# A hybrid streaming encoder step: gates a unit later, norm sums behind the mLSTM gates, rows turned among v's units

## What is computed

```python
def _trunk(x, p, cache, w):                      # cut
    for li in range(2):
        hn = _rmsnorm(h, norm_mix_g[li])
        # layer 0: RG-LRU and windowed attention behind one input projection
        # layer 1: mLSTM (matrix memory, chunks of 64)
        h = h + mixer(hn)
        h = h + _swiglu(_rmsnorm(h, norm_ffn_g[li]), ffn_w_in[li], ffn_w_out[li])
        h = h + jax.nn.sigmoid(h @ ple_w_gate[li]) * (p[li] @ ple_w_proj[li])
    return _rmsnorm(h, final_g), states

def _rglru(u, h0, w_r, b_r, w_i, b_i, lam):      # layer 0, u is behind a causal convolution
    r = jax.nn.sigmoid(_block_diag(u, w_r) + b_r)
    i = jax.nn.sigmoid(_block_diag(u, w_i) + b_i)
    log_a = -8.0 * r * jax.nn.softplus(-lam)
    a = jnp.exp(log_a)
    bx = jnp.sqrt(-jnp.expm1(2.0 * log_a)) * (i * u)
    # h[t] = a[t] * h[t-1] + bx[t]

proj = _rmsnorm(x, norm_mix_g[1]) @ w_in         # layer 1
u, v, o, gates = jnp.split(proj, [1024, 2048, 3072], axis=-1)
ig, lf = gates[..., :4] + b, jax.nn.log_sigmoid(gates[..., 4:] + b)
```

## Time and profile before

| | us |
|---|---|
| median of 3 runs | 2843.92 (2843.08 to 2844.82) |
| the profiled execution | 2844.14 |
| its span, first to last instruction | 2842.4 |
| PE busy | 2729.6 (96%) |
| DVE busy | 1476.1 (52%) |
| POOL busy | 949.9 (33%) |
| ACT busy | 600.7 (21%) |
| mean granted TensorE clock | 0.982 |

### The profile page before, as it was taken

One profiled execution on the slowest core, in us unless ns is written; L12 is line 12 of the kernel. 1 busy time (PEld: TensorE's weight loads), 2 busy tenths in 40 slices (PEclk: granted clock), 3 DMA queues, 4 the chain that ended last, 5 costly groups with the idle time before them and its releaser, 6 DMA issues.

```text
span 2842.4 us, 40945 instructions
## 1 busy us (share of the span) xinstructions
PE 2729.6 (96%) x17240; PEld 2672.7 (94%) x17240; DVE 1476.1 (52%) x2332; ACT 600.7 (21%) x1266; POOL 949.9 (33%) x439
## 2 busy tenths in 40 slices
PE   7999999999999999998999988799999999999996
PEld 7798899999999999998999977699999999999996
DVE  7956474444444444658663056546444444444565
ACT  3434331000000000223122145312000000000042
POOL 5222044433333333333433310024433333333430
PEclk9999999999999999999999999899999999999998
DMA  4101011111111111113122221301111111111111
GB/s 145 33 23 61 32 60 51 47 46 52 46 45 45 45 45 45 45 45 122 45 75 85 91 78 45 151 30 51 54 45 45 45 45 45 45 45 45 53 38 61
DMA packets 57830, 160.09 MB, mean 56 GB/s; under 512 B 7340, under 2 KB 28332, under 8 KB 56368
## 3 DMA queue, kind: packets, MB, share of 16 engines
q1 hardware_dynamic: 31056, 109.79, 12.3%
q10 hardware_dynamic: 26592, 47.70, 4.6%
HBM read 137.07 MB, written 20.40 MB: 55 GB/s over the span
## 4 chain that ended last, share of the span: by engine, by line
PE 90%; DVE 6%; ACT 3%; issue 1%; DMA 0%; ACTq 0%; DVEq 0%
PE ps L413 28%; PE ps L415 28%; PE ps L414 28%; PE ps L819 1%; PE ps L619 1%; PE ps L589 1%; PE ps L856 1%; DVE xl L907 1%; DVE uc L1178 1%; DVE hb L1489 1%; PE ps L601 0%; DVE cs L1463 0%; PE ps L858 0%; ACT kw L1926 0%; DVE rstd L900 0%
## 5 line engine op out<-in xcount | busy, mean ns | idle before, releaser
L413 PE MATMUL ps<-xh,wh 128*128 128x352 f32 x3432 | 1122.3, 327 | 21.3 <-DVE xl L907 14.3
L414 PE MATMUL ps<-xl,wh 128*128 128x352 f32 x3432 | 1114.4, 325 | 0.0
L415 PE MATMUL ps<-xh,wl 128*128 128x352 f32 x3432 | 1114.0, 325 | 0.0
L464 POOL TENSOR_TENSOR wh<-raw,seeds 128x1024 fp32r<-128x1024 f32 x208 | 422.3, 2030 | 1807.6 <-PE ps L415 1779.9
L413 PEld LDWEIGHTS ps<-xh,wh 128*128 128x128 f32 x3432 | 651.8, 190 | 26.2 <-issue 13.9
L414 PEld LDWEIGHTS ps<-xl,wh 128*128 128x128 f32 x3432 | 651.9, 190 | 2.1 <-issue 0.3
L415 PEld LDWEIGHTS ps<-xh,wl 128*128 128x128 f32 x3432 | 651.7, 190 | 0.0
L466 POOL TENSOR_TENSOR wl<-raw,wh 128x1024 fp32r<-128x1024 f32 x208 | 529.5, 2546 | 16.3
L1023 DVE TENSOR_TENSOR tmpa<-ps,rstd 128x352 f32<-128x352 f32 x132 | 69.1, 524 | 719.0 <-PE ps L415 710.8
L413 PE MATMUL ps<-hh,wh 128*128 128x352 f32 x1056 | 340.4, 322 | 0.0
L415 PE MATMUL ps<-hh,wl 128*128 128x352 f32 x1056 | 340.0, 322 | 0.0
(11 more groups left out here) (263 smaller groups left out, 2497.6 us busy)
## 6 DMA issues: line engine op xcount, KB each, us to landing
raw<-wstream SPq DMA_DIRECT2D x208, 512.0 KB, 3.6
vod<-stage ACTq DMA_DIRECT2D x72, 128.0 KB, 1.9
vb<-vod ACTq DMA_DIRECT2D x9, 512.0 KB, 4.0
ob<-vod ACTq DMA_DIRECT2D x9, 512.0 KB, 3.7
x<-xT ACTq DMA_DIRECT2D x3, 1408.0 KB, 11.7
x<-xT ACTq DMA_DIRECT2D x2, 2112.0 KB, 8.2
xsave<-x ACTq DMA_DIRECT2D x1, 4224.0 KB, 11.4
x<-xsave ACTq DMA_DIRECT2D x1, 4224.0 KB, 14.4
```

The source lines that it names most:

```text
L413: pe.matmul(out, whi, mhi, start=first, stop=False)
L414: pe.matmul(out, whi, mlo, start=False, stop=False)
L415: return pe.matmul(out, wlo, mhi, start=False, stop=last)
L464: pool.tensor_tensor(hi, raw[:, r, :], zero, ALU.add).then_inc(hi_made, 1)
```

## The change

Five edits:

1. Layer 0: `lru_gates(0)` stands after unit 12 instead of 11, and POOL splits block 6 only once conv(0) is done (`uc_ready`).
2. ScalarE's `gates(t)` begins with a one-column sigmoid that waits for nothing, ahead of the waits.
3. The transposes of v alternate between banks 6 and 7, so that only the ninth waits for a copy.
4. Norm ni = 2: all three sums stand behind the three units of the mLSTM gates' block; roots and reciprocals move behind the last highs and lows. POOL splits B1_GATE + 1 once the lows of two tiles are done, B1_GATE + 2 once all are.
5. `rows_to_columns` stands inside the first pair of v's blocks, ahead of its fourth token tile, instead of ahead of the pair.

```diff
-            later = {B0_FFN + 2: "ffn0", B1_FFN + 2: "ffn1"}
+            later = {B0_FFN + 2: XLN["ffn0"] + KT * NT, B1_FFN + 2: XLN["ffn1"] + KT * NT,
+                     B1_GATE + 1: XLN["mix1"] + KT * 2, B1_GATE + 2: XLN["mix1"] + KT * NT}
                 if b in later:
-                    pool.wait_ge(xl_ready, 1 + XLN[later[b]] + KT * NT)
+                    pool.wait_ge(xl_ready, 1 + later[b])
+                if b == 6:
+                    pool.wait_ge(uc_ready, 1)
@@ tail_phase (PE)
-                    if u == first or u == first + 4:
+                    if ni != 2 and u in (first, first + 4):
                         norm_sum(ni, (u - first) // 4)
@@ dense (PE)
-                    if tt == 1 and sums is not None:
-                        norm_sum(sums, NT - 1)
@@ transpose_v (PE)
-                    if j == 4:
+                    if j == 8:
                         pe.wait_ge(v_ready, 1)
-                    if j == 8:
-                        pe.wait_ge(v_ready, 2)
-                    mm = pe.transpose(ps[0:n, 7, (j % 4) * P:(j % 4 + 1) * P], vt[:, j * P:j * P + n], ident[:, :])
+                    mm = pe.transpose(ps[0:n, 6 + j // 4 % 2, (j % 4) * P:(j % 4 + 1) * P], vt[:, j * P:j * P + n], ident[:, :])
@@ IN0 loop (PE)
-                if u == 11:
+                if u == 12:
                     pe.wait_ge(m0_in, 16 * 5)
-                if u in (11, 14, 17):
-                    lru_gates((11, 14, 17).index(u))
+                if u in (12, 14, 17):
+                    lru_gates((12, 14, 17).index(u))
@@ layer 1 (PE)
-            dense(B1_GATE % NW, B1_GATE, FREE0["g1"] - 6, OFF["g1"], XLN["mix1"], 2)
+            dense(B1_GATE % NW, B1_GATE, FREE0["g1"] - 6, OFF["g1"], XLN["mix1"])
+            for tt in range(NT):
+                norm_sum(2, tt)
             dense_loop("u1", B1_U, KT)
-            (the rows' 53 matmuls and their two waits)
+            def rows_to_columns():
+                (the same)
                         for j in range(CH):
+                            if pair == 0 and j == 3:
+                                rows_to_columns()
@@ tail_phase (DVE)
-                        if u == 20:
+                        if u == 20 and ni != 2:
                             rstd_of(ni, 0)
-                    rstd_of(ni, 1)
-                    rstd_of(ni, 2)
+                    for tt in range(0 if ni == 2 else 1, NT):
+                        rstd_of(ni, tt)
@@ tail_norm (ACT)
-                    if u == 19 or u == 23:
+                    if ni != 2 and u in (19, 23):
                         root(ni, (u - 19) // 4)
-                        root(ni, 2)
+                        for tt in range(0 if ni == 2 else 2, NT):
+                            root(ni, tt)
@@ gates (ACT)
             def gates(t):
+                act.activation(seeds[:, 7:8], seeds[:, 0:1], ACT.Sigmoid)
                 if t >= 2:
                     act.wait_ge(h_ready, t - 1)
@@ values (ACT)
-                    (copies of v from bank 7)
+                    (copies of v from bank 6 + j, the ninth from bank 6)
```

More of the change, by code:

```diff
@@ L506, in tail_phase, with dense @@
                     first = 18 if ni < 4 else 17
-                    if u == first or u == first + 4:
+                    if ni != 2 and u in (first, first + 4):
                         norm_sum(ni, (u - first) // 4)
-            def dense(slot, b, free, bank0, xl_at=None, sums=None):
+            def dense(slot, b, free, bank0, xl_at=None):
                 pe.wait_ge(raw_free, split_count(b))
                 for tt in range(NT):
-                    if tt == 1 and sums is not None:
-                        norm_sum(sums, NT - 1)
                     pe.wait_ge(acc_free, free + tt + 1)
@@ L770, in _ @@
             ple(0, B0_PLE)
-            dense(B1_GATE % NW, B1_GATE, FREE0["g1"] - 6, OFF["g1"], XLN["mix1"], 2)
+            dense(B1_GATE % NW, B1_GATE, FREE0["g1"] - 6, OFF["g1"], XLN["mix1"])
+            for tt in range(NT):
+                norm_sum(2, tt)
             dense_loop("u1", B1_U, KT)
[L775 to L788, removed]
+            def rows_to_columns():
+                pe.wait_ge(rows_ready, 1)
+                pe.wait_ge(c_in, 16 * 4)
+                for cc in range(CH):
+                    for q in range(4):
+                        r = (0, 5, 4, 1)[q]
+                        pe.transpose(ps[:, 6, (cc * 4 + q) * 4:(cc * 4 + q + 1) * 4],
+                                     rows[:, r, cc * P:(cc + 1) * P], ident[0:4, 0:4])
+                for h in range(H):
+                    mm = pe.matmul(ps[:, 6, 256 + CH * h:256 + CH * (h + 1)], sel[:, h, :], rsmall[:, 32:32 + CH],
+                                   start=True, stop=True)
+                for cc in range(CH):
+                    n = P if cc < CH - 1 else TS
+                    mm = pe.transpose(ps[0:n, 6, 320 + 4 * cc:324 + 4 * cc], rstd[0:4, cc * P:cc * P + n], ident[0:4, 0:4])
+                mm.then_inc(cols_done, 1)
             for half in range(2):
@@ L1727, in values @@
                 if j < 2:
-                    act.activation(vtok[:, 4 * j + 1:4 * j + 5, :].rearrange("p a d -> p (a d)"), ps[:, 7, :],
+                    act.activation(vtok[:, 4 * j + 1:4 * j + 5, :].rearrange("p a d -> p (a d)"), ps[:, 6 + j, :],
                                    ACT.Copy).then_inc(v_ready, 1)
                 else:
-                    act.activation(vtok[0:TS, 10, :], ps[0:TS, 7, 0:P], ACT.Copy).then_inc(v_ready, 1)
+                    act.activation(vtok[0:TS, 10, :], ps[0:TS, 6, 0:P], ACT.Copy).then_inc(v_ready, 1)
             gates(0)
```

## The result

The changed kernel takes 2823.26 us (median of 4 runs, 2817.26 to 2824.80), the kernel before 2843.62 (4 runs, 2843.08 to 2844.82). The ratio is 0.992, with a 95% interval of 0.991 to 0.993: faster by 20 us. The prediction said 2820.7, between 2813.5 and 2829.5. The profiled execution took 2824.18 us, with a span of 2822.4, so it is 19.96 us shorter than the one of before (2844.14).

The account below looks back on a forecast made before the run. PE was busy 2729.6 of 2842.4 us, so only its waits and low-clock time could be won. Gains of 9.6 + 10.7 + 3.0 = 23.3 us gave 2820.7 us, range 2813.5 to 2829.5.

Parts of the forecast that it names:

- Part C: mLSTM rows to columns behind three of v's units: wait covered, small matmuls and next unit at full clock, 9.6 us gained.
- the small matmuls at 2.4 GHz: Among v's units: the 53 small matmuls would take 3.6 us at full clock instead of 6.5.
- rival 4: Four new pauses or thin stretches each bring a low-clock period costing about 6.8 us; slower, 2848 us; chance 0.02.
- lower bound, 6.7: Rows to columns: gain of 6.7 us if the small matmuls keep 6.5 us because their pace is not the array's.
- Part B: Layer 1's norm sums behind the mLSTM gates, splits held: 12.8 us lost time removed, less new waits; 10.7 us gained.
- The 0.3 us for the third norm sum: Layer 1's norm: the third sum needs the first root, so PE would wait 0.3 us.
- Part A: Layer 0's gates: moved splits only move their cost; gains from table loads and v's transposes, 3.0 us in all.
- Rival 1: Layer 0's gates pay in full, log1p and conv(1) not held by the moved splits: 2816.1 us; chance 0.13.
- rival 3: Layer 0's first gates stay bound by something other than conv(0), gaining nothing: 2823.7 us; chance included in the forecast's 0.70.
- conv(1): Layer 0: block 8's split delays this convolution's end to 88.8 from 85.2; PE waits 7.5 us before gates 1.
- the row: Table loads: the trace shows 1.28 us each without the drain; the forecast used this, not the skill's extra 1.38.
- Rival 2: New waits replace those removed in layer 1's norm and the rows to columns: 2828.2 us; chance 0.13.

Follow-up runs that it names:

- e1_rows: Kernel before with only the rows' small matmuls moved inside v's first pair of blocks, behind three units: 2838.11 us, ratio 0.9975.
- e4_norm_nohold: Kernel before with only the layer 1 norm sums moved behind the mLSTM gates, without the two waits that hold GpSimd's splits: 2844.86 us, ratio 0.9997.
- e9_24: Changed kernel with the split of block B1_GATE + 1 held until all 24 lows are done instead of 16: 2818.21 us, ratio 0.9907.
- e5_nohold6: Changed kernel without GpSimd's wait for conv(0) ahead of splitting block 6: 2821.06 us, ratio 0.9916.
- e2_norm: Kernel before with only the layer 1 norm sums moved behind the mLSTM gates and the two splits held: 2836.55 us, ratio 0.9967.
- e3_gates: Kernel before with only the layer 0 changes (gates 0 later, block 6 held, sigmoid table ahead, two banks for v's transposes): 2840.46 us, ratio 0.9986.
- r14_after: The changed kernel measured again, unaltered, on the chip of three later kernels: 2822.12 us, ratio 0.9919 against the kernel before.
- e13_later_only: Changed kernel with layer 0's gates 0, 1, 2 after units 12, 15, 18 and v's transposes after 22, log1p left in place: 2819.73 us, ratio 0.9912.
- e12_best: Changed kernel with early log1p, later gates and transposes, block B1_GATE + 1 held until 24 lows, small matmuls in three groups: 2815.02 us, ratio 0.9893.
- e11_later: Changed kernel with log1p early, layer 0's gates 0, 1, 2 after units 12, 15, 18 and v's transposes after 22: 2816.86 us, ratio 0.9904.

## Why the prediction was right, and where it was not

The forecast of 2820.7 missed the median by 2.6 us. It is right in the mechanism of each part and, for the last microseconds, by luck: the parts gained 1.5 us more than predicted, and stretches that the prediction left out took 4.9.

**Part C** was right in each term: no wait, 3.7 us for the small matmuls (3.6 predicted), 3.0 for the unit behind (2.9), 9.4 in all (9.6). That is the profile; e1_rows and six more show that the clock mostly falls there, so that 6.4 to 7.9 is what this part usually gives. The weak step is "the small matmuls at 2.4 GHz": the prediction gave no chance of its own to a clock that falls within them (it stood among the four places of rival 4). Its own lower bound, 6.7, came from another mechanism and is close by luck.

**Part B** was right in mechanism: e4_norm_nohold and e9_24 show that the splits stretch the lows, that holding them is what pays, and that the one left in the way costs PE between 1 and 1.6 us (1.8 predicted, from 0 to 4.3). The 0.3 us for the third norm sum did not come, since the root was early enough: the three sums run without a pause, and the hoisted table load stands 6.6 us ahead of the first root. Timelines of PE and of ACT:

```profile
1308.21 0.43 PE L413 MATMUL ps<-xh,wh 128*128 128x352 f32 x1 [1.05 <-DVE xl L913]
...
1311.28 2.32 PE L492 MATMUL ps<-sqsum,ones 128*128 128x352 f32 x6
```

```profile
1305.47 1.28 ACT L1549 ACT_TABLE_LOAD   x1
1312.07 0.55 ACT L1549 ACTIVATE rt<-ps,vecs 128x352 f32<-128x352 f32 x1 [5.32 <-PE ps L492]
```

11.4 against 10.7: the two waits were 1.05 us smaller than predicted. Some of it is lost again behind the sums, where the first matmul of u takes 0.59 us in place of 0.32 and u's first unit 4.15 in place of 3.88 (so in every kernel whose norm sums stand there, and in no other).

**Part A** was right in its main claim, that the moved splits only move their cost: the product of gates 0 starts 1.0 us earlier (0.5 predicted) though conv(0) ends 5 earlier, and e5_nohold6 shows the hold to be worth 0.2 to 0.4. Rival 1, part A in full, falls with that; so does rival 3, since gates 0 follow unit 12 without a wait and the part gained 4 us. The step that failed is conv(1): it was to end at 88.8 and ended at 85.6 (87.3, less 1.69), so the wait before gates 1 is 4.2 us and not 7.5. The log1p came as predicted, but the convolution met less of the split than the prediction had charged. Its 3.6 us fit both instructions of block 8's split; the last three instructions of conv(1) began 0.5 us earlier than the prediction implies and the split 0.3 later (80.1 and 81.7, corrected), so only the first of the two (83.35 in the timeline) got in between, and they took 5.55 us instead of 4.04. The second (86.29) had to wait for the last of conv(1) in turn: it took 3.24 us, where it takes 2.40 alone. PE is 2.0 us ahead behind gates 1 (0.5 predicted), 2.9 at unit 21 (1.6 predicted for this place), and 4.0 behind gates 3. PE in the changed kernel:

```profile
87.39 0.96 PE L542 MATMUL ps<-uc,lbd 128*128 128x353 f32 x1 [4.18 <-DVE uc L1184]
...
126.61 0.28 PE L552 MATMUL ps<-ident,vt 128*32 128x128 f32 x1 [3.39 <-ACT vtok L1736]
```

The second row is the ninth transpose alone: the one round trip left takes 3.4 us, nearly as much as the two of before (2.8 + 0.7). PE's lead grows by only 0.2 us from unit 18 to unit 21, so edit 3 shows next to no gain of its own here. The table load of gates 3 stands ahead of its wait, as predicted (ACT's timeline; it was at 141.85 behind the wait in the earlier trace rows), and gives 1.1 us (1.3):

```profile
127.22 1.28 ACT L1711 ACT_TABLE_LOAD   x1
```

The Trainium skill, "ScalarE: Activation LUTs", section What ACT_TABLE_LOAD costs, would by its figure have added an estimated 2.8 us for a drain with these two loads. Gates 3 gained 1.1 us, less than the load alone, so the trace doesn't show the drain; the row was the right choice.

**What was not in the sum** are the stretches outside: +1.7 at the input stage, +1.5 in u's units, +2.1 in the mLSTM chunks. The first and the last come mainly from low-clock stretches that fall differently in each execution. At the input stage the profiles had 0, 3.4 or 6.8 us of them, and were 0 to 4.3 us late, in kernels that have the same code up to there (e2_norm +1.7, e3_gates +3.9, e5_nohold6 about 0, r14_after +3.0). Four of them (e3_gates, r14_after, e13_later_only, e12_best) have there also a wait of 1.1 to 1.4 us for one of VectorE's lows that the others don't have, so it isn't all the clock. The stretch between parts A and B scatters as much: the same code there gave -0.4 in the changed kernel, but -3.9 in r14_after, -4.7 in e5_nohold6 and +1.7 in e11_later, with 20.5, 13.7, 13.7 and 23.9 us at half clock (20.5 before). In the profile of r14_after all that lies outside the parts costs 1.0 us instead of 4.9. The prediction took the profile of before, with no low clock at the input stage, as the base, and so its sum began from a favourable start; nothing in one profile could show that, and the runs' own spread of 1.7 us hid it (on the other chips the kernel before spread over 6 to 12 us).

Of the 1.5 in u's units 0.3 is the first unit behind the norm sums; the other 1.2 is not the change's. A unit of 24 matmuls takes 3.83 us before and 3.88 after (159.5 and 161.7 ns a matmul), both at full clock; in 50 us the table counts 316 and 311 of them. The tables by stretches of the kernel before, of the changed one and of e3_gates:

```profile
1350.00:1400.00 50.00, 50.00 (x316) 50.00 (x315) 42.32 (x29) 6.35 (x18) 28.03 (x10) 1.00 0.14 43
```

```profile
1350.00:1400.00 50.00, 50.00 (x311) 50.00 (x311) 37.87 (x24) 6.30 (x17) 26.31 (x10) 1.00 0.15 43
```

```profile
1350.00:1400.00 50.00, 50.00 (x311) 50.00 (x311) 41.64 (x28) 6.24 (x18) 26.30 (x10) 1.00 0.15 43
```

e3_gates and e1_rows have the code of the kernel before in this layer up to here, and 311 too, as have all the other profiles (311 or 312). So in this stretch the one profile of the kernel before is the exception. The two rhythms themselves are in every profile; here they are in two stretches of layer 0 of the kernel before, and the other thirteen profiles have the same two there:

```profile
440.00:490.00 50.00, 50.00 (x316) 50.00 (x315) 21.67 (x24) 5.98 (x12) 18.15 (x8) 1.00 0.13 43
600.00:650.00 50.00, 50.00 (x312) 50.00 (x311) 15.06 (x24) 4.49 (x9) 13.29 (x6) 1.00 0.13 42
```

What makes the rhythm is open.

Rival 2 (2828.2) and rival 4 (2848) did not come, though rival 4's mechanism did: after the pause of 4.2 us before gates 1 the clock is at 0.5 for 6.8 us, and at the small matmuls it usually falls. There it costs 1.5 us (3.4 us of it) or 3.0 (6.8 us of it), not the 6.8 that the prediction charged for a period of 13.

## What to carry to other kernels

When two engines exclude each other, a stall that is moved isn't a stall that is gone: ask which instruction the moved work meets next, and put it where the other engine is idle or waited for by nobody; here the holds paid in part B (8.4 of 11.4 us), where the splits were not needed soon, and hardly in part A (0.2 to 0.4), where they met the next chain. When an engine waits for a chain that runs late, giving it a unit of independent work first can be worth the wait and also the clock behind it (part C: 4.7 us of wait, and 1.7 to 4.7 of clock); check then each later wait of the same chain, since one of them (here conv(2)) takes the role. Lay the two traces side by side by the same matmul and read the steps: a local gain is checked to a few tenths that way, or to 0.8 where the clock fell differently, while whole times scatter by several microseconds. And one profile of the kernel before is one draw: to know what a stage usually costs, take it from more than one.

## What the runs showed of the hardware

- The exclusion of VectorE and GpSimd works by whole instructions, down to tiny ones: an operation on 4 columns that takes 0.16 us alone took 2.18 beside a split instruction of 2.36 us, and eight took 3.61 instead of 1.54. VectorE's instructions with one input in PSUM were not stretched beside the same splits (0.48 us for 320 columns at 69.24, inside GpSimd's instruction at 68.92). The Trainium skill, "SBUF — State Buffer", section Terms, says of the shared port pair that the other engine fully blocks for the whole instruction; the rows agree.
- At 53 small matmuls (45 of 4 columns, 8 of 9; 3.7 us at full clock) PE's granted clock fell from 2.4 to 1.2 GHz without any gap, PE busy throughout: among them in four of eight profiles, for 6.8 us, and 0.8 to 1.5 us behind them in three, for 3.4 us. It fell in neither of the two where they were spread between three units of v. A busy share of 100% in the table doesn't mean that the clock stays.
- The same code had 0, 3.4 or 6.8 us at half clock in the input stage, and 13.7 to 23.9 us between parts A and B.
- Matmuls of 352 columns at a granted clock of 1.00 ran in two rhythms, one every 159.5 or every 161.7 ns. Each profile has both, in different stretches; in layer 1's u the same code had the first in one profile and the second in thirteen.
